# Sample attention of a decoder step: the last two output products of a sequence behind its values' products, and the clearing of sums and weights behind the first page

## The reference, cut to what matters

```python
def diff_attn_sample(q, k, v, lam, past_k, past_v):
    s = jnp.concatenate([diff_scores(q, past_k),
                         jnp.where(causal, diff_scores(q, k), NEG_INF)], axis=-1)
    w = diff_weights(s, lam)            # softmax of both halves, p0 - lam * p1
    return (jnp.einsum("bhqk,bkhe->bqhe", w[..., :n_past], past_v)
            + jnp.einsum("bhqk,bkhe->bqhe", w[..., n_past:], v))
```

## Time and profile before

| | us |
|---|---|
| median of 3 runs | 2308.75 (2307.97 to 2312.24) |
| the profiled execution, its own time | 2319.28 |
| its span, first to last instruction | 2317.6 |
| PE busy | 2146.9 (93%) |
| DVE, ACT, POOL busy | 909.0, 632.8, 319.4 |
| the stage of the change | about 2017 to 2317.6 |
| granted TensorE clock, mean over the span | 0.961 of full |

### The profile page before, as it was taken

One profiled execution on the slowest core, in us unless ns is written; L12 is line 12 of the kernel. 1 busy time (PEld: TensorE's weight loads), 2 busy tenths in 40 slices (PEclk: granted clock), 3 DMA queues, 4 the chain that ended last, 5 costly groups with the idle time before them and its releaser, 6 DMA issues. The chain is left out here.

```text
span 2317.6 us, 47084 instructions
## 1 busy us (share of the span) xinstructions
PE 2146.9 (93%) x20794; PEld 1416.6 (61%) x20794; DVE 909.0 (39%) x1765; ACT 632.8 (27%) x1433; POOL 319.4 (14%) x279
## 2 busy tenths in 40 slices
PE   7999999999999999998997999998899799489997
PEld 4577585675866857754554555555567566356664
DVE  4253462543634525322323133053222588623332
ACT  5321222223213222222214211122222366311111
POOL 0000020110200201111001030320010366201110
PEclk9999999999999999998989999999899799789998
DMA  7100010000100100007002120200002000357663
GB/s 257 30 20 11 10 40 20 30 21 10 30 21 15 36 20 30 21 15 261 22 1 105 53 87 28 103 9 10 18 28 82 1 1 1 146 204 234 215 202 101
DMA packets 52798, 147.84 MB, mean 64 GB/s; under 512 B 11459, under 2 KB 20995, under 8 KB 51316
## 3 DMA queue, kind: packets, MB, share of 16 engines
q1 hardware_dynamic: 42612, 103.97, 13.2%
q0 software_dynamic: 9984, 40.87, 5.1%
HBM read 123.58 MB, written 21.24 MB: 62 GB/s over the span
## 5 line engine op out<-in xcount | busy, mean ns | idle before, releaser
L755 PE MATMUL psum<-xT,rw_w 128*128 128x384 f32 (+1 forms) x1152 | 397.7, 484 | 2.8 <-PEq L169 2.8
L755 PEld LDWEIGHTS psum<-xT,rw_w 128*128 128x128 f32 x1152 | 206.1, 189 | 119.9 <-issue 9.4
L2020 PE MATMUL psum<-spare,xT 128*128 128x384 f32 (+1 forms) x432 | 143.3, 494 | 1.5 <-PEq L169 1.5
L2020 PE MATMUL psum<-kvq_w,xT 128*128 128x384 f32 (+1 forms) x432 | 140.6, 487 | 0.0
L1298 DVE SCALAR_TENSOR_TENSOR rwkv_xs<-psum,rwkv_pc,rwkv_xsc 128x64 f32<-128x64 f32 x90 | 25.5, 284 | 238.9 <-PE psum L974 238.9
L2020 PEld LDWEIGHTS psum<-spare,xT 128*128 128x128 f32 (+1 forms) x432 | 80.4, 187 | 62.8 <-issue 13.6
L2020 PEld LDWEIGHTS psum<-kvq_w,xT 128*128 128x128 f32 (+1 forms) x432 | 79.0, 184 | 61.3 <-issue 11.2
L1103 ACT COPY rwkv_r_sb<-psum 128x64 f32<-128x64 f32 x96 | 20.4, 213 | 328.1 <-PE psum L956 295.1
L723 POOL DMA_DIRECT2D out<-rwkv_s x6 | 5.7, 954 | 754.7 <-ACT rwkv_out_p L1124 754.7
L2099 DVE TENSOR_REDUCE kvq_ss<-kvq_sq 128x6 f32<-128x384 f32 (+1 forms) x36 | 19.9, 552 | 201.8 <-ACT kvq_sq L2062 201.6
L2423 PE MATMUL psum<-V,yT 128*128 128x512 f32 x192 | 97.5, 633 | 0.0
(11 more groups left out here) (437 smaller groups left out, 4032.7 us busy)
## 6 DMA issues: line engine op xcount, KB each, us to landing
xT<-in_cache_k SPq DMA_DIRECT2D x64, 384.0 KB, 3.9
samp_vp<-in_cache_v POOLq DMA_DIRECT2D x64, 384.0 KB, 4.7
rw_w<-in_w_in SPq DMA_DIRECT2D x28, 512.0 KB, 3.7
front_w<-in_mem_w_kv SPq DMA_DIRECT2D x2, 2048.0 KB, 14.2
x_rows<-in_x_p SPq DMA_DIRECT2D x8, 512.0 KB, 13.7
h<-in_x_p SPq DMA_DIRECT2D x8, 512.0 KB, 13.2
residual<-h POOLq DMA_DIRECT2D x8, 512.0 KB, 3.0
xT<-in_w_out SPq DMA_DIRECT2D x2, 1536.0 KB, 13.2
```

The costliest lines, as they stand in the source:

```text
L755: mm = pe.matmul(out, w[:, load % 2, k, :], xT[:, k, a:b], start=(k == 0), stop=(k == KC - 1))
L2020: mm = pe.matmul(bank[0:r, j % 6, 0:W], xT[:, k, n * P:n * P + r], w[i % 2][:, k, :], start=(k == 0), stop=(k == KC - 1))
```

## The change

On PE, the piece of products behind page 7 of each sequence (between.pe) moves from before that sequence's last scores to behind values(b - 1), directly before turn_weights(b); sequence 0 has no earlier values, and there the product that starts the accumulation (L2588) stands in their place, moved from the stage's start, behind a wait for the new semaphore zeroed. On DVE, the addition that belongs to that piece moves from before fill_queries to behind joined (L2673). The clearing of the weights and of new_probs and the computing of coef move from the stage's start to behind the first page's copy; the clearing of the weights signals zeroed instead of going through link, and in sequence 0 DVE waits for zeroed before it writes the weights.

```diff
--- before.py
+++ after.py
@@ -2492,9 +2492,9 @@
         k_loaded = [st.sem(f"k_loaded{i}") for i in range(KR)]
         v_loaded = [st.sem(f"v_loaded{i}") for i in range(VR)]
         (pages_loaded, q_ready, turned, act_out, dve_out, k_used, s_mm, mx_ready, exp_ready, join_ready, w_mm, w_ready, o_mm,
-         sq_ready, ss_ready, rs_ready, o_ready, o_turned, y_ready, v_used, dve_chain, act_chain) = st.sems(
+         sq_ready, ss_ready, rs_ready, o_ready, o_turned, y_ready, v_used, zeroed, dve_chain, act_chain) = st.sems(
             "pages_loaded q_ready turned act_out dve_out k_used s_mm mx_ready exp_ready join_ready w_mm w_ready o_mm "
-            "sq_ready ss_ready rs_ready o_ready o_turned y_ready v_used dve_chain act_chain")
+            "sq_ready ss_ready rs_ready o_ready o_turned y_ready v_used zeroed dve_chain act_chain")
         between.begin(st)
         block = st.block()
         scores_of = wide[0:R, 0:PAGES * P]
@@ -2584,9 +2584,6 @@
                 mm.then_inc(o_mm, 1)
 
 
-            pe.wait_ge(q_ready, 1)
-            pe.matmul(out_of, weights[:, 0, 0:4, :].rearrange("p h x -> p (h x)"), KT[:, DH - 1, 0:512], start=True, stop=False)
-
             for b in range(B):
                 for pg in range(PAGES):
                     g = b * PAGES + pg
@@ -2595,11 +2592,16 @@
                     if pg % 2:
                         for done in range(max(pg - 2, 0), pg):
                             scores(b * PAGES + done)
-                    between.pe(pe, g)
+                    if pg < PAGES - 1:
+                        between.pe(pe, g)
                 scores(b * PAGES + PAGES - 1)
                 new_scores(b)
                 if b >= 1:
                     values(b - 1)
+                else:
+                    pe.wait_ge(zeroed, 1)
+                    pe.matmul(out_of, weights[:, 0, 0:4, :].rearrange("p h x -> p (h x)"), KT[:, DH - 1, 0:512], start=True, stop=False)
+                between.pe(pe, b * PAGES + PAGES - 1)
                 turn_weights(b)
             values(B - 1)
             pe.wait_ge(o_ready, 1)
@@ -2632,11 +2634,6 @@
         def _(dve):
             link = Chain(dve, dve_chain)
             link(nc.vector.memset(flat[:, at + 2560:at + 2560 + 2 * DH * QG], 0.0))
-            link(nc.vector.memset(weights[:, :, :, :], 0.0))
-            link(nc.vector.memset(new_probs[:, :], 0.0))
-
-            link(nc.vector.scalar_tensor_tensor(out=coef[:, :], in0=isc[0:R, 1:2], scalar=lam[0:R, 0:1], in1=isc[0:R, 0:1],
-                                                op0=ALU.mult, op1=ALU.add))
 
             def fill_queries(b):
                 for c in range(2):
@@ -2655,7 +2652,13 @@
                     if g >= TR:
                         dve.wait_ge(k_used, g - TR + 1)
                     nc.vector.tensor_copy(kT[:, g % TR, 1, :], bank[:, 5, 0:H3 * P]).then_inc(dve_out, 1)
-                    between.dve(dve, g)
+                    if g == 0:
+                        link(nc.vector.scalar_tensor_tensor(out=coef[:, :], in0=isc[0:R, 1:2], scalar=lam[0:R, 0:1], in1=isc[0:R, 0:1],
+                                                            op0=ALU.mult, op1=ALU.add))
+                        link(nc.vector.memset(new_probs[:, :], 0.0))
+                        nc.vector.memset(weights[:, :, :, :], 0.0).then_inc(zeroed, 1)
+                    if pg < PAGES - 1:
+                        between.dve(dve, g)
                 if b + 1 < B:
                     fill_queries(b + 1)
                 dve.wait_ge(s_mm, b + 1)
@@ -2671,6 +2674,9 @@
                 link(nc.vector.reciprocal(ls[:, 0:1], ls[:, 0:1]))
                 link(nc.vector.tensor_tensor(ls[:, 0:1], ls[:, 0:1], coef[:, :], ALU.mult))
                 nc.vector.tensor_scalar(joined[:, :], join[0:R, :], ls[:, 0:1], None, ALU.mult).then_inc(join_ready, 1)
+                between.dve(dve, b * PAGES + PAGES - 1)
+                if b == 0:
+                    dve.wait_ge(zeroed, 1)
                 if b >= 1:
                     dve.wait_ge(o_mm, b)
                     nc.vector.memset(weights[:, :, :, (b - 1) % 4 * TS:((b - 1) % 4 + 1) * TS], 0.0)
```

## The result

The changed kernel takes 2288.73 us (median of 4 runs, 2286.22 to 2295.1) against 2310.49 us before (median of 4, 2307.97 to 2313.81): 21.8 us less, ratio 0.9903 with a 95% interval of 0.9887 to 0.9919. The forecast was 2291.4 us, range 2285.5 to 2300.5. The profiled execution after has its own time at 2286.22 us, 33.06 less than the one before (2319.28). Not all of that is the change: the last output scaling of the stage before (L2341) starts at 2004.63 instead of 2015.62 us, and up to there nothing was edited. These 10.99 us are how one execution differs from another.

A forecast was written before the change was run, and what follows sets the result against it. PE's waits for DVE's joined before turn_weights, 12.8 us, bound the kernel in a few places. Waits of 10.41 us plus 6.94 of clock, 17.35 us, off the median 2308.75 gave 2291.4 us, range 2285.5 to 2300.5.

The forecast's parts named there:

- stage's start to the fourth key page's turn: Before the first pages: work moved off DVE and PE is absorbed by PE's 2.77 us key-page wait; gain 0.
- The softmax starts earlier: DVE, sequences 1 to 6: maximum at 2085.98 instead of 2088.70, so joined ends 2.72 us earlier.
- remark on PE alone: PE before turn_weights: moving only PE's piece ends at the same 2091.67 whichever way the piece lies.
- The waits of sequences 1 to 7: PE before turn_weights: waits for joined all go, 7.29 us in sequences 1 to 6 and 0.40 in 7.
- The order of neighbours: PE's piece among narrower products: as many changes of form as before, cost 0, 1.6 us either side for eight sequences.
- The clock of sequences 2, 3 and 5: PE behind these turns: none of the three half-clock stretches remains, gain 5.04 us, bounds 0 and 8.5.
- the first rival: Waits alone: turning products, not waits, let the clock fall, so it falls as often as now; 2298.3 us, chance 0.20.
- the place in time decides: PE's turns in sequences 1 to 6 sit at the edge; where they lie in time decides whether the clock falls.
- The clock of sequence 0: PE round sequence 0's turn: one half-clock stretch of 1.7 us replaces 3.60, gain 1.90 us, bounds 0 and 3.60.
- Before turn 0: PE in sequence 0: turn_weights 2.72 us earlier, with 1.40 of the 5.15 us wait remaining.
- The last values: PE behind sequence 7's turn: 0.88 us wait and half-clock stretch both stay, clock gain 0, bounds 0 and 1.7.
- The place of the ten microseconds: Profiled execution, 10.5 us above the median with nothing showing where: the gain is subtracted from the median, 2308.75.

The follow-up runs named there:

- the filler: Kernel before plus two products with unread results in PE's 1.2 us wait before turn_weights, sequences 1 to 6: 2308.87 against 2313.33 us (0.9977).
- The two kernels with a wait of 0.4 us: Changed kernel with PE's piece behind turn_weights, 2299.25 us (0.9933); kernel before with only DVE's page-7 addition moved behind joined, 2302.91 us (0.9954).

## Why the prediction was right

By places, in the two profiled executions (forecast us, measured us):

| stretch | forecast | before | after | gain |
|---|---|---|---|---|
| stage's start to the fourth key page's turn | 0 | 18.92 | 17.51 | 1.41 |
| from there to turn 0 | 2.72 | 23.05 | 18.66 | 4.39 |
| turn 0 to turn 1 | 3.12 | 35.29 | 33.43 | 1.86 |
| turn 1 to turn 6 | 11.11 | 163.46 | 150.38 | 13.08 |
| turn 6 to turn 7 | 0.40 | 30.87 | 30.07 | 0.80 |
| turn 7 to the end | 0 | 30.39 | 29.82 | 0.57 |
| sum | 17.35 | | | 22.11 |

**The softmax starts earlier: right.** L2666 starts 0.20 us behind L2665 and that behind the new scores. Both moves were needed for the whole: PE's alone is 57 us slower, DVE's alone gives about half. The prediction's remark on PE alone, that it ends at the same place whichever way the piece lies, was far too kind: it left out that the addition would take the piece's lateness in front of the softmax.

**The waits of sequences 1 to 7: right.** All gone. The margin of joined, forecast at 1.57 us, is 1.42 (2072.81 to 2074.23).

**The order of neighbours: mis-sized.** It was taken at 0, with 0.2 us a sequence to either side. Where no fall comes, the distance was 31.68 less a wait of 1.21, so 30.47 us of work; the addition alone gives the same 30.87 - 0.40 = 30.47. After it is 30.07. The new order saves 0.40 us of PE time in each sequence, 2.0 us between turns 1 and 6. The prediction's count of changes of form was wrong: it said as many as before, but from the last scores to the turn there were three (into the piece, out of it to scores, and from values to the turn) and now there are two. The count doesn't give the size by itself: with the piece behind the turn, and still fewer changes up to the next page, it is 30.59 - 0.40 = 30.19 us. Why the order costs what it does stays open. Timeline of the kernel before, sequence 1:

```profile
2083.94 1.07 PE L2553 MATMUL psum<-xT 128*32 128x128 f32 x24
2084.94 1.98 PE L2423 MATMUL psum<-KT,y_m 128*128 128x512 f32 x4
2086.86 0.64 PE L2553 MATMUL psum<-xT 128*32 128x128 f32 x12
2087.32 0.25 PE L2561 MATMUL psum<-KT,xT 128*32 128x8 f32 x9
```

The parts: last scores and the two pages' before them in one run to the first new scores, 1.34 us after (2066.79 to 2068.13) against 1.46 before, piece and scores set apart (1.00 from the two pages' scores at 2083.94 to 2084.94, and 0.46 from 2086.86 to 2087.32); from the values' end at 2072.48 to the turn 1.75 instead of the piece's 1.92; and the turn to L2685 2.16 instead of 2.27.

**The clock of sequences 2, 3 and 5: right,** with the cause narrowed but not fully separated. 13.08 less 5 x 1.21 of waits and 2.0 of order leaves 5.03, forecast 5.04. There were 10 falls in 18 turns with the wait against 0 in 42 without, and the filler shows that wide products in the wait are enough to keep the clock while the turn stays where it was. The turning products as such were the first rival; it falls, since they are the same in all these kernels. But in those 42 turns and in the filler kernel two things came together: no idle time, and wide products directly ahead of the turn. The two kernels with a wait of 0.4 us have neither, and there the falls are 2 in 12. Which of the two keeps the clock isn't shown; a turn directly behind the values, without idle time, was not run. The prediction's remark that the place in time decides isn't shown either. For this kernel the rule cited beside the first rival, from the Trainium skill, "TensorE: Matmul & The Clock Gate", section "HAM oscillation — how this bites in real kernels", doesn't hold: it puts falls down to longer idle gaps, and here a gap of 1.2 us, filled, gave 4.5 us back.

**The clock of sequence 0: mis-sized.** Forecast was one stretch of the short kind left and 1.90 us won. Measured, turn 0 to 1 is 33.43 us, in the changed kernel again 33.43 and 33.40, which is about 3.35 above 30.07, against 3.60 before. So 0.25 us was won. Behind the turn the stretch lasted 7.6 us before (2057.59 to 2065.2; the first 2.5 of its 10.1 us lay in the wait, where they cost nothing) and 6.8 us now (2042.4 to 2049.2), not 3.4 as the forecast took. Two pieces there remove it: 30.18 and 30.18 us.

**Before turn 0: mis-sized.** 4.39 us instead of 2.72, since PE waited only 0.95 us for the fourth key page and no half-clock stretch followed it, where the earlier trace rows had 2.77 us and the stretch. That is 1.6 us, and with the 1.41 above it comes from when the page arrives, which the prediction took as fixed; it varied from 17.0 to 20.0 us over the profiles. These 3 us are thus partly chance of the two executions compared. The forecast step itself comes out well where no such stretch disturbs it: the kernel before's second profile takes 21.51 us from the fourth page to turn 0 (2025.74 to 2047.25), the changed kernel's three 18.66, 18.90 and 18.90, so 2.6 to 2.9 us less. The wait left ahead of turn 0 is 1.57 us, forecast 1.40.

**The last values: mis-sized.** The stretch at half clock was forecast to stay; in the changed kernel's three profiles it came in none, but pages of values were then late, by 1.0, 1.2 and 0.7 us in all. This new wait takes back part of what the clock gives. Over all profiles the stretch came in three of six with a wait of 0.40 us ahead of turn 7, and in one of seven with none. From turn 7 on 0.57 us was won.

**The place of the ten microseconds.** They lie ahead of the stage, in code that is the same. Taking the difference from the median was right.

**How much of the agreement is luck.** The forecast gain of 17.35 us was 4.76 short of the profiles' 22.11. The misses have both signs: before turn 0 1.67 too little and at the stage's start 1.41 (both partly chance), the order 2.8 too little in seven distances, the last values 0.57 too little, and the clock of sequence 0 1.65 too much. Against the kernel before's second profile (300.31 us) the changed kernel's three win 20.0 to 20.7 us.

## What to carry to other kernels

A wait is removed at the start of the chain that ends it: find the first instruction on each engine that stands ahead of the chain without belonging to it, and move it behind, on all engines that share it. PE's move alone turned 22 us of gain into 57 of loss, DVE's alone kept about half of the gain. Wide products moved into a wait can be worth more than the wait, namely the slow stretches that followed it as well; here these made 5.0 of 22.1 us, and 1.6 more by chance of a load. Where whole-program times spread by 10 us and more, a stage's own time from a fixed instruction shows differences of 4 us that medians don't.

## What was not expected of the hardware

- With waits of 0.40 us ahead of the turn, and no wide products directly ahead of it, the clock still fell to 0.50 behind it in 2 of 12 turns, each costing 1.6 to 1.7 us; with 1.2 us it was 10 of 18.
- The same pieces (128x512), scores and values (32 weight columns) and turning products cost 0.40 us less of PE time a sequence in another order.
- The fourth key page arrives anywhere from 17.0 to 20.0 us after the stage's start with the same instructions ahead of it on its queue.
